# Three-pass u blocks, and a w stage with the weights as stationary: one change to a two-block transformer kernel

## The reference, cut to what matters

```python
def peer(x, w_q, sub_keys_1, sub_keys_2, u_tab, v_tab):   # per block of 128 tokens
    q = (xb @ w_q) ...
    s1, s2 = q[..., 0, :] @ k1.T, q[..., 1, :] @ k2.T      # 128 keys each
    ... top 16 of each, top 16 of their 256 sums -> idx, g = softmax(top_s)
    u_sel = jnp.take(u_tab, idx, axis=0)                   # (T, heads, 16, D)
    h = jnp.einsum('bthkd,btd->bthk', u_sel, xb)
    a = jax.nn.gelu(h) * g
    return jnp.einsum('bthk,bthkd->btd', a, jnp.take(v_tab, idx, axis=0))
```

## Time and profile before

| | |
|---|---|
| time, median of 3 runs | 1540.49 us (1537.07 to 1542.85) |
| the profiled execution | 1540.41 us, span 1538.6 us |
| TensorE busy with matmuls | 1510.0 us, 98% |
| VectorE / ScalarE / GpSimd busy | 1106.3 / 766.1 / 334.5 us |
| u stage | 852.8 to about 1224 us |
| w stage | 1228.6 to 1532.3 us |

### The profile page before, as it was taken

One profiled execution on the slowest core, in us unless ns is written; L12 is line 12 of the kernel. 1 busy time (PEld: TensorE's weight loads), 2 busy tenths in 40 slices (PEclk: granted clock), 3 DMA queues, 4 the chain that ended last, 5 costly groups with the idle time before them and its releaser, 6 DMA issues.

```text
span 1538.6 us, 26335 instructions
## 1 busy us (share of the span) xinstructions
PE 1510.0 (98%) x10162; PEld 1390.0 (90%) x10162; DVE 1106.3 (72%) x2153; ACT 766.1 (50%) x1562; POOL 334.5 (22%) x240
## 2 busy tenths in 40 slices
PE   6999999999999999999999999999999899999998
PEld 6999997799999977899999999999999877777777
DVE  6766678767666775656768895666666588988887
ACT  7554555555545555544444113444433356666665
POOL 1111113202111120100016010222222134343331
PEclk9999999999999999999999999999999999999999
DMA  5555556445555564344554477888888889999996
GB/s 187 185 187 182 184 182 220 140 138 165 186 185 183 174 197 144 127 148 135 174 175 124 155 279 242 290 287 299 292 293 296 279 280 343 341 335 327 350 339 214
DMA packets 95851, 344.68 MB, mean 224 GB/s; under 512 B 10664, under 2 KB 11952, under 8 KB 95728
## 3 DMA queue, kind: packets, MB, share of 16 engines
q1 hardware_dynamic: 77296, 275.89, 53.4%
q0 software_dynamic: 18432, 67.12, 12.3%
HBM read 341.92 MB, written 1.05 MB: 223 GB/s over the span
## 4 chain that ended last, share of the span: by engine, by line
PE 85%; DVE 6%; DMA 3%; ACT 3%; issue 2%; POOL 1%; SPq 0%; DVEq 0%; ACTq 0%; POOLq 0%
PE ps L1002 84%; DMA RAW<-wall 3%; DVE WL L434 2%; ACT WH L606 1%; DVE YS L1521 1%; DVE HL L1521 1%; POOL FS L520 1%; DVE XT L1518 0%; DVE SS L1521 0%; DMA XT<-xt 0%; PE ps L1158 0%; ACT HH L624 0%; POOL SM L487 0%; DVE MX L1712 0%; PE ps L1177 0%
## 5 line engine op out<-in xcount | busy, mean ns | idle before, releaser
L434 DVE TENSOR_TENSOR WL<-RAW,WH 128x1024 fp32r<-128x1024 f32 x361 | 442.1, 1225 | 188.2 <-ACT WH L606 167.9
L606 ACT ACTIVATE WH<-RAW 128x1024 fp32r<-128x1024 f32 x354 | 373.0, 1055 | 257.3 <-PE ps L1002 243.3
L1002 PE MATMUL ps<-XT,RAW 128*128 128x192 f32 x2048 | 344.1, 327 | 0.1
L1002 PEld LDWEIGHTS ps<-XT,RAW 128*128 128x128 f32 x2048 | 331.5, 190 | 0.5 <-issue 0.4
L1002 PE MATMUL ps<-HH,WH 128*128 128x256 f32 x976 | 279.9, 287 | 0.3 <-DVE WL L434 0.3
L1002 PE MATMUL ps<-HL,WH 128*128 128x256 f32 x976 | 276.1, 283 | 0.0
L1002 PE MATMUL ps<-HH,WL 128*128 128x256 f32 x976 | 275.9, 283 | 0.0
L1002 PE MATMUL ps<-WH,GG 128*128 128x512 f32 x768 | 267.5, 400 | 5.0 <-DVE GG L1518 4.6
L1002 PE MATMUL ps<-WL,GG 128*128 128x512 f32 x512 | 203.8, 398 | 0.0
L1002 PEld LDWEIGHTS ps<-HH,WH 128*128 128x128 f32 x976 | 186.8, 191 | 2.9 <-issue 2.4
L1002 PEld LDWEIGHTS ps<-HL,WH 128*128 128x128 f32 x976 | 187.0, 192 | 1.0 <-issue 1.0
(11 more groups left out here) (271 smaller groups left out, 2449.3 us busy)
## 6 DMA issues: line engine op xcount, KB each, us to landing
RAW<-wall SPq DMA_DIRECT2D x510, 512.0 KB
B<-rel SPq DMA_DIRECT2D x4, 768.0 KB, 6.0
DEC<-con SPq DMA_DIRECT2D x4, 384.0 KB, 4.3
XT<-xt SPq DMA_DIRECT2D x4, 256.0 KB, 5.6
UB<-utab,IDXU POOLq DMA_INDIRECT x64
VB<-wall,IDXV POOLq DMA_INDIRECT x64, 8.1
WIN<-con SPq DMA_DIRECT2D x1, 768.0 KB, 8.6
out<-XT SPq DMA_DIRECT2D x2, 256.0 KB, 2.6
```

Source lines behind the costliest of these rows:

```text
L434: ins = eng.tensor_tensor(wl, RAW[:, b % NRAW, :], wh.bitcast(F), ALU.subtract)
L606: act.activation(halves(b)[0], RAW[:, b % NRAW, :], ACT.Copy).then_inc(s_hi, 1)
L1002: return pe.matmul(o, l, r, start=start, stop=stop, skip_group_check=True)
```

## The change

Two things are changed together. First, 58 blocks of the u stage (those with 36 <= c < 124 and c not a multiple of 3, the set THREE) are taken by halves: `high` on ScalarE and `low` on VectorE for each, and `block()` with XH and XL, the halves of x for the 192 dense tokens, made once before. The other 70 stay direct. Second, in the w stage the halves of the weight block are stationary, 128 columns at a time, and the halves of the activations GH and GL (192 tokens) move: 8 times three matmuls a block. The sums then lie transposed, width in the partitions, two slices of 192 in each of banks 0 to 3; they are started with x through the identity, and at the end copied to OT, turned by TensorE and copied out. XH and XL lie where VB lies, so the v gathers start only after the last block of THREE, and after all u gathers. VectorE's low moves behind one_hots() and dot().

```diff
+THREE = {UP + c for c in range(36, 124) if c % 3}
+DIRECT = set(range(UP, WP)) - THREE
...
-            GG = sb("GG", [128, 2, 448], R, ph)
-            UB, VB = sb("UB", [128, NGET, D], F, ph), sb("VB", [128, NGET, D], F, ph)
+            GH, GL = sb("GH", [128, 2, ND], R, ph), sb("GL", [128, 2, ND], R, ph)
+            UB = sb("UB", [128, NGET, D], F, ph)
+            with ExitStack() as sub:
+                XH, XL = sb("XH", [128, KD, ND], R, sub), sb("XL", [128, KD, ND], R, sub)
+            VB = sb("VB", [128, NGET, D], F, ph)
...
+            for k in range(KD):
+                pool.wait_ge(s_hh, 48 + k + 1)
+                pool.tensor_tensor(XL[:, k, :], XT[:, k, DENSE], XH[:, k, :].bitcast(F), ALU.subtract).then_inc(s_hl, 1)
             candidates(0)
             candidates(1)
             pool.wait_ge(s_idx, 4)
-            for j in range(NGET):
+            for j in range(NSP):
                 gather_u(j)
-            for j in range(NGET):
-                gather_v(j)
-            for j in range(NGET, NSP):
-                gather_u(j)
-            for j in range(NGET, NSP):
+            pool.wait_ge(s_blk, max(THREE) + 1)
+            for j in range(NSP):
                 gather_v(j)
...
+                if l >= 8:
+                    act.wait_ge(s_xn, 8)
+                    act.activation(XH[:, l - 8, :], XT[:, l - 8, DENSE], ACT.Copy).then_inc(s_hh, 1)
...
-                    if UP + c + 2 >= WP:
+                    if UP + c + 2 not in DIRECT:
                         high(UP + c + 2)
...
-                act.activation(GG[:, c % 2, 0:64], BIG3[:, c, 0:64], ACT.Copy)
-                act.activation(GG[:, c % 2, 256:448], BIG3[:, c, :], ACT.Copy).then_inc(s_gh, 1)
+                act.activation(GH[:, c % 2, :], BIG3[:, c, :], ACT.Copy).then_inc(s_gh, 1)
...
-            for k in range(2):
-                act.wait_ge(s_acc, 12 + k + 1)
-                act.activation(UB[0:NSP, 0, 512 * k:512 * k + 512], bank[k][64:128, :], ACT.Copy).then_inc(s_mlow, 1)
+            for k in range(4):
...
+                act.activation(OT[:, 2 * k:2 * k + 2, :].rearrange("p k t -> p (k t)"), bank[k][:, 0:2 * ND], ACT.Copy).then_inc(s_ot, 1)
+            for h in range(2):
+                act.wait_ge(s_rtr, 2 + h + 1)
+                act.activation(XO[0:NSP, h, :], bank[6 + h][0:NSP, :], ACT.Copy).then_inc(s_xe, 1)
...
+            for k in range(KD):
+                mm(sums(k), IDENT, XT[:, k, DENSE], k % 2 == 0, False)
...
-                direct(UP + c, bank[4 + (c + 1) % 2][:, 0:ND])
+                if UP + c in DIRECT:
+                    direct(UP + c, bank[4 + (c + 1) % 2][:, 0:ND])
+                else:
+                    block(UP + c, bank[4 + (c + 1) % 2][:, 0:ND], XH, XL, 48 if UP + c == min(THREE) else None)
...
-                both, low, high = GG[:, s, 0:128], GG[:, s, 128:256], GG[:, s, 320:448]
-                for k in range(2):
-                    d = slice(512 * k, 512 * k + 512)
-                    mm(bank[k][:, :], both, wh[:, d], False, False)
-                    ins = mm(bank[k][:, :], both, wl[:, d], False, c == 127)
...
-                    ins = mm3(bank[2 + k][:, :], high, low, wh[:, d], wl[:, d], False, c == 127)
...
+                for k in range(KD):
+                    ins = mm3(sums(k), wh[:, c128(k)], wl[:, c128(k)], GH[:, s, :], GL[:, s, :], False, c == 127)
...
+            for k in range(KD):
+                if k % 2 == 0:
+                    pe.wait_ge(s_ot, k // 2 + 1)
+                pe.transpose(bank[4 + k // 4][:, c128(k % 4)], OT[:, k, NSP:ND], IDENT)
+                ins = pe.transpose(bank[6 + k // 4][0:NSP, c128(k % 4)], OT[:, k, 0:NSP], IDENT)
...
-                low_if_mine(UP + c + 2)
                 if c in QUAD_AT:
                     one_hots(QUAD_AT[c])
                 if c in DOT_SLOT:
                     dot(DOT_SLOT[c])
+                low_if_mine(UP + c + 2)
```

More of the change, by code:

```diff
@@ L99 @@
 ATT, MIX, PQ, UP, WP = AT["qk", 8], AT["sqk", 0], AT["pq", 0], AT["u", 0], AT["w", 0]
-DIRECT = set(range(UP, WP))
+THREE = {UP + c for c in range(36, 124) if c % 3}
+DIRECT = set(range(UP, WP)) - THREE
 _ring = [b for b in range(N_BLOCKS) if b not in OWN and b not in DIRECT]
@@ L323, in build @@
             GS, DOTS, AS = (sb(n, [128, NSP], F, ph) for n in ("GS", "DOTS", "AS"))
-            ZERO = sb("ZERO", [128, 64], F, ph)
         MROT = GB[:, :, :].rearrange("p k t -> p (k t)").rearrange("p (g t c) -> p g t c", g=2, t=2)
@@ L330, in build @@
         XO = XT[:, :, :].rearrange("p k t -> p (k t)").rearrange("p (b c) -> p b c", b=4)
+        OT = UB[:, :, :].rearrange("p j d -> p (j d)")[:, 0:KD * ND].rearrange("p (k t) -> p k t", k=KD)
         ONEH = OHS[:, :].rearrange("p (s a w i t) -> p s a w i t", s=2, a=4, w=2, t=2)
@@ L402, in build @@
         d_u, d_v = ([sem(f"{n}{i}") for i in range(NGET)] for n in ("d_u", "d_v"))
-        s_zero, s_xe, s_xsp, s_xs, s_idx, s_dot, s_act, s_wgt, s_vs, s_half, s_ys, s_mlow = (sem(n) for n in (
+        s_zero, s_xe, s_xsp, s_xs, s_idx, s_dot, s_act, s_wgt, s_vs, s_half, s_ys, s_ot = (sem(n) for n in (
             "s_zero", "s_xe", "s_xsp", "s_xs", "s_idx", "s_dot", "s_act", "s_wgt", "s_vs", "s_half", "s_ys",
-            "s_mlow"))
+            "s_ot"))
         s_oh, s_pd, s_pp, s_bt, s_mm, s_mc, s_gel, s_tmg, s_xo = (sem(n) for n in (
@@ L473, in sync_program @@
             sp.dma_start(out[0, 0:NSP, :], YS[0:NSP, :]).then_inc(d_out, 16)
[L474 to L480, removed]
+            for h in range(2):
+                o = slice(512 * h, 512 * h + 512)
+                sp.wait_ge(s_xo, h + 1)
+                sp.dma_start(out[1, :, o], XO[:, 2 + h, :]).then_inc(d_out, 16)
+                sp.wait_ge(s_xe, 2 + h + 1)
+                sp.dma_start(out[0, PAIRED, o], XO[0:NSP, h, :]).then_inc(d_out, 16)
             sp.wait_ge(d_out, 80)
@@ L581, in pool_program @@
             rows_of_wall = wall.rearrange("b p k -> (b p) k")
-            pool.memset(ZERO[:, :], 0.0).then_inc(s_zero, 1)
+            pool.wait_ge(s_pw, 6)
+            pool.memset(YS[NSP:128, :], 0.0).then_inc(s_zero, 1)
             pool.wait_ge(s_zero, 1)
-            pool.memset(YS[NSP:128, :], 0.0).then_inc(s_zero, 1)
-            pool.wait_ge(s_zero, 2)
             for b in range(PQ + 3, UP - 2):
                 low_if_mine(b + 2)
+            for k in range(KD):
+                pool.wait_ge(s_hh, 48 + k + 1)
+                pool.tensor_tensor(XL[:, k, :], XT[:, k, DENSE], XH[:, k, :].bitcast(F), ALU.subtract).then_inc(s_hl, 1)
             candidates(0)
@@ L994, in scalar_program @@
                     act.activation(XS[0:NSP, :], YS[NSP:128, :], ACT.Copy).then_inc(s_half, 1)
-            for k in range(2):
-                act.wait_ge(s_acc, 12 + k + 1)
-                act.activation(UB[0:NSP, 0, 512 * k:512 * k + 512], bank[k][64:128, :], ACT.Copy).then_inc(s_mlow, 1)
+            for k in range(4):
+                if k < 3:
+                    act.wait_ge(s_acc, 12 + k + 1)
+                else:
+                    act.wait_ge(s_blk, N_BLOCKS)
+                act.activation(OT[:, 2 * k:2 * k + 2, :].rearrange("p k t -> p (k t)"), bank[k][:, 0:2 * ND], ACT.Copy).then_inc(s_ot, 1)
+            for h in range(2):
+                act.wait_ge(s_rtr, 2 + h + 1)
+                act.activation(XO[0:NSP, h, :], bank[6 + h][0:NSP, :], ACT.Copy).then_inc(s_xe, 1)
         def tensor_program(pe):
@@ L1408, in tensor_program, with sums @@
             enter(5)
[L1412 to L1419, removed]
+            def sums(k):
+                return bank[k // 2][:, ND * (k % 2):ND * (k % 2) + ND]
+            for k in range(KD):
+                mm(sums(k), IDENT, XT[:, k, DENSE], k % 2 == 0, False)
             def sparse_residual():
@@ L1500, in tensor_program @@
                 wh, wl = halves(b)
-                both, low, high = GG[:, s, 0:128], GG[:, s, 128:256], GG[:, s, 320:448]
-                for k in range(2):
-                    d = slice(512 * k, 512 * k + 512)
-                    mm(bank[k][:, :], both, wh[:, d], False, False)
-                    ins = mm(bank[k][:, :], both, wl[:, d], False, c == 127)
[L1506 to L1509, removed]
-                    ins = mm3(bank[2 + k][:, :], high, low, wh[:, d], wl[:, d], False, c == 127)
-                    if c == 127 and k == 0:
+                for k in range(KD):
+                    ins = mm3(sums(k), wh[:, c128(k)], wl[:, c128(k)], GH[:, s, :], GL[:, s, :], False, c == 127)
+                    if c == 127 and k in (1, 3, 5):
                         ins.then_inc(s_acc, 1)
                 ins.then_inc(s_blk, 1)
+            for k in range(KD):
[3 more added lines that the diff above has]
+                ins = pe.transpose(bank[6 + k // 4][0:NSP, c128(k % 4)], OT[:, k, 0:NSP], IDENT)
+                if k % 4 == 3:
+                    ins.then_inc(s_rtr, 1)
         def vector_program(dve):
@@ L2145, in summed @@
                     dve.wait_ge(s_xe, 2)
```

(7 more changed lines are left out.)

## The result

| | before | after |
|---|---|---|
| time, median | 1539.63 us (4 runs, 1537.07 to 1542.85) | 1597.10 us (4 runs, 1594.59 to 1598.38) |
| ratio | | 1.037, 95% interval 1.0346 to 1.0394 |
| span of the profiled execution | 1538.6 us | 1595.4 us |
| start of the sums, up to the first u block | 852.8 us | 850.4 us |
| u stage | 371.5 us | 390.3 us |

The spans differ by 56.8 us, and the stages account for it: -2.4 + 18.8 - 0.6 + 41.2 - 0.3 = 56.7. So three quarters of the loss lie in the w stage and one third in the u stage, less a little at the edges.

A forecast was written before the change was run, and what follows sets the result against it. TensorE's matmuls were taken as the bound; 1540.4 + 50 (w stage) + 2.8 (u matmuls) + 21 (copy waits) - 2.5 (start) + 1 (gap) = 1612.7, rounded to 1612; range 1578 to 1640 us (0.65), or to 1655 (0.8).

The forecast's parts named there:

- The direction: Whole kernel: the change makes it slower, chance 0.85; same 0.05, faster 0.1.
- the deciding term: w stage: an fp32r matmul with 192 columns costs its weight load, 0.114 us; +50 us, bounds +41 and +68.
- Rival A: Both stages: the 128-column fp32r load hides behind the previous matmul, step 0.091 us; total 1511 us; chance 0.1.
- TensorE in the u stage: 58 three-pass u blocks: 2.736 us each for 2.69 direct, +2.8 us, bounds -1 and +11.
- The waits behind the copy: u stage: ScalarE's new copy and its transfer delay weighted() and the gate matmuls; +21 us, bounds 0 and +42.
- Start of the sums: Before the u stage: 16 records of 192 columns replace the earlier matmuls; -2.5 us, bounds -1 and -3.
- Gap: Between the stages: later v gathers beside the first w transfer, less up to one dot; +1 us, bounds -1 and +3.
- Tail: End of the kernel: copy, four transposes and copy replace copy, two sums and copy; 0, bounds -1 and +1.
- VectorE: u stage: 58 lows of 1.22 us fit, VectorE busy 240 of 260 us; taken at nothing.

The follow-up runs named there:

- The wide runs: High half loaded once for 384 moving columns, against the kernel before: 29 u blocks 1536.24 us; 44 blocks 1539.45 us; 44 with 22 lows on GpSimd 1565.81 us.
- the run with mixed columns: Changed kernel with 192 token columns moving in w blocks 0 to 7, 160 up to block 67, 64 from there: 1737.1 us.

## Why the prediction was right

- **The sum.** 1597 us lies inside the range, 15 under the forecast of 1612: some 9 of it in the w stage, 5 in the u stage and 1.6 in the gap. All three sums were taken too high; no large errors cancel in the total.
- **The direction and the deciding term.** The w stage was forecast at +50 us and measured +41.2, the lower bound. The mechanism was right, the size a little off: I took 0.114 us, the middle between float32 rows, and it is 0.1123. The rows that priced nothing but loads (0.111 and 0.113 in the earlier trace rows, 0.11 in the earlier trace rows) were nearer than the float32 matmuls with 64 columns (0.115). Over 3072 matmuls 0.0017 us is 5 us; the other 4 are the 303.7 us of the old stage against the 300.2 that I subtracted: its small gaps and its slow start belonged into the difference.
- **Rival A** took 0.091 us for what the moving side costs. Two measured steps lie near it, 0.089 with 96 stationary columns and 0.09 for the narrow matmul behind the wide one. It was wrong in that the load isn't hidden behind a matmul of 192 columns. Its bound by VectorE and the transfers was right too: 2.3 us a block, and 298 us over 128 blocks is 2.33. The rule of the Trainium skill ("TensorE: Matmul & The Clock Gate", section "LDWEIGHTS (loading the stationary operand)"), columns over 1.2, gave 107 ns, and the full-clock runs show 112. The other rule of the page, for an isolated matmul, N / 2.4 + 2.5 ns ("Back-to-back issue gap"), is shown by no run here: 82.5 ns for 192 columns isn't reached even with the shorter load.
- **TensorE in the u stage**: forecast +2.8, measured +3.9, and the price of a direct block behind the forecast was off. The kernel before has this row, and its gate matmuls follow at 1102.69, so a direct block costs 2.62 us there and not 2.69:

```profile
1097.44 5.42 PE L1002 MATMUL ps<-XT,RAW 128*128 128x192 f32 x32
```

Busy time over count is more than the step, since the last record of a row is counted with its whole length. A three-pass block took 2.74 us (1060.44 to 1063.18). That the difference came out near the forecast is in part luck: the direct block ahead of a three-pass one is 0.13 us shorter, 2.52 us, and the forecast hadn't counted on that.

- **The waits behind the copy**: forecast +21 (0 to 42). The place and the cause were right. The trace's idle time of TensorE in the u stage, 8.8 us, shows only a part of them, since a wait hides under the tail of the record before it. The same step in the changed kernel and in the run with weighted() first:

```profile
1063.18 2.79 PE L1012 MATMUL ps<-XT,RAW 128*128 128x192 f32 x16
1066.01 0.85 PE L1012 MATMUL ps<-OHS 128*128 128x128 bf16 x12
```

```profile
1039.04 2.79 PE L1012 MATMUL ps<-XT,RAW 128*128 128x192 f32 x16
1041.66 0.85 PE L1012 MATMUL ps<-OHS 128*128 128x128 bf16 x12
```

Both blocks are busy for 2.79 us, but the gate matmuls start 2.83 us after the block's start in the first and 2.62 in the second: 0.21 us late, of which the chain shows 0.04 as idle. Counted like this through the stage, the gate matmuls are late in 28 places, by 13.3 us in all. Five places, of 0.7 to 3.3 us, make up 8.5 of it, and the other 23 lie between 0.15 and 0.32. The forecast was 0.3 us in 16 places and 1.0 us in 16. With 3.9 us of TensorE's own steps and 1.6 of the clock these are the 18.8 us. In the run with weighted() first 0.4 us is left of the 13.3, and 3.7 us of waits ahead of three-pass blocks, for VectorE's low, come in their place: 12.9 + 1.6 - 3.7 is the gain of 10.8.

- **The clock** was missing from the forecast. After the wait of 1.80 us (to 1102.18) it was at half for some 3 us, while after the wait of 3.13 us (to 960.53) it stayed full:

```profile
950.00:960.00 10.00, 7.39 (x69) 1.00 0.93 324
960.00:1000.00 40.00, 39.27 (x353) 1.00 0.72 259
...
1099.00:1104.00 5.00, 3.19 (x27) 0.83 0.71 264
1104.00:1112.00 8.00, 8.00 (x64) 0.89 0.48 164
```

So the length of a wait alone isn't what decides. In the run with 64 moving columns, whose u stage is the same kernel's, TensorE stood 1.79 us up to 959.19, and there the clock was 0.59 between 960 and 964.

- **Start of the sums**: -2.5 forecast, -2.4 measured. **Gap**: +1 forecast, -0.6 measured in the changed kernel, but +1.0 with the u part alone; both inside the bounds. **Tail**: 0 and -0.3.
- **VectorE** was taken at nothing in the u stage, and that held: 216.90 of 260 us busy, while I had counted 240. The stage is longer, so the stretch holds 54 of the 58 lows, but also only 54 dots for 59 and 43 groups of one-hots for 47. The wide runs show how near it was: at 222.77 of 250 it makes up most of the chain.

## What to carry to other kernels

In a row of fp32r matmuls of one form each has two prices, that of its weight load, which goes by the stationary columns, and that of its moving columns, and the step is the larger: with 128 stationary columns 64, 160 and 192 moving columns all cost 0.112 us (the moving side would take over at some 240, an estimate by the line; 256 cost 0.120). So counting the moving columns alone would have missed this. The price of the load can be read ahead of the change from the short matmuls in the trace, as a step from start to start. And before an operation that waits for a transfer is added to an engine's fixed order, look at what is queued behind it: here the swap of two calls was worth 10.8 us. Idle time alone would have undercounted it: short waits hide under the record before them, and the step to the next start shows them.

## What the runs showed that I had not expected

- The load goes by TensorE's clock: the step is 0.112 us at full clock and 0.213 us, nearly twice that, at half, at 64, 160 and 192 moving columns alike.
- The clock was at half for long stretches in which TensorE never stood still and had a load for every matmul. After the same gap of some 4 us it rose with 192 moving columns in the changed kernel (0.87 in the stretch from 1248 to 1252 us, 1.00 after) and stayed at 0.50 for over 600 us with 160 and with 64. In the run with mixed columns it stayed at 1.00 with 160, and at 64 it fell. Two of the experiments took 300 us longer by it, with fewer columns to move. Each of these cases is one execution.
- A narrow matmul behind a wide one costs 0.09 us, under its load's 0.112: the load starts under the wide one, 0.17 us ahead of its own matmul, so what counts is the pair.
